# Weights as the stationary operand for the first modulation, and moving operands of high and low columns side by side

## The reference

```python
silu_c = jax.nn.silu(c)[:, None, :]
silu_cc = jax.nn.silu(c_ctx)
for i in range(DEPTH):                      # DEPTH = 4
    sh_a, sc_a, g_a, sh_m, sc_m, g_m = jnp.split(silu_c @ mod_w[i] + mod_b[i], 6, axis=-1)
    h_lat = modulate(x_lat, norm_mix_g[i], sh_a, sc_a)
    ...                                     # the same for the context with silu_cc
    y_lat = fourier_mixer | diff_attention_mixer | mla_mixer
    x_lat = x_lat + g_a * y_lat
    x_lat = x_lat + g_m * sq_relu_mlp(modulate(x_lat, norm_mlp_g[i], sh_m, sc_m), mlp_w1[i], mlp_w2[i])
```

## Time and profile before

| what | value |
|---|---|
| median of three runs | 2016.28 us (2011.03 to 2016.95) |
| the profiled execution's own time | 2013.53 us |
| its span, first to last instruction | 2011.8 us |
| mean granted clock of TensorE | 0.984 |
| PE, DVE, ACT busy | 1921.9, 1531.0, 1018.4 us |
| bytes moved, mean rate | 346.67 MB, 172 GB/s |

### The profile page before, as it was taken

The page is one execution under the profiler, slowest core; times in us unless marked ns, Lnnn a source line. Parts: engine busy times, 40 slices in busy tenths (PEclk is TensorE's granted clock), DMA queues, the critical chain, the costliest instruction groups (busy, mean ns, idle before and its releaser), DMA issues.

```text
span 2011.8 us, 31051 instructions
## 1 busy us (share of the span) xinstructions
PE 1921.9 (96%) x11602; PEld 1684.5 (84%) x11602; DVE 1531.0 (76%) x2619; ACT 1018.4 (51%) x1721; POOL 22.5 (1%) x40
## 2 busy tenths in 40 slices
PE   6889999999999999999999777999999999999998
PEld 4687888889787888888888667999999999997886
DVE  3689888887667758777777588788887667876796
ACT  5353323245666656232333577655555546655685
POOL 0200000000000000000000100000000000000000
PEclk9999999999999999999999899999999999999999
DMA  7936455541211234557675220677645555426795
GB/s 291 321 119 232 165 209 188 188 168 48 84 64 63 67 112 139 169 186 244 236 244 158 58 73 27 227 268 261 207 135 189 168 169 168 134 67 236 260 354 195
DMA packets 265319, 346.67 MB, mean 172 GB/s; under 512 B 24167, under 2 KB 234962, under 8 KB 263778
## 3 DMA queue, kind: packets, MB, share of 16 engines
q1 hardware_dynamic: 265186, 344.90, 51.2%
HBM read 343.81 MB, written 1.06 MB: 171 GB/s over the span
## 4 chain that ended last, share of the span: by engine, by line
PE 75%; DVE 10%; ACT 6%; issue 5%; SPq 1%; DMA 1%; DVEq 0%; ACTq 0%
PE bank L1847 23%; PE bank L1848 23%; PE bank L1849 23%; PE bank L2663 2%; DVE w_lo L2818 2%; PE bank L2653 1%; ACT p_raw L1401 1%; ACT p_raw L1389 1%; DVE p_all L3297 1%; ACT norm L1157 1%; ACT w_hi L1064 1%; ACT mp_raw L1569 1%; DVE x L2886 1%; DVE neg_max L3306 1%; DVE norm L2844 1%
## 5 line engine op out<-in xcount | busy, mean ns | idle before, releaser
L2818 DVE TENSOR_TENSOR w_lo<-w_raw,w_hi 128x1024 fp32r<-128x1024 f32 x449 | 545.6, 1221 | 51.6 <-ACT w_hi L1064 24.9
L1064 ACT ACTIVATE w_hi<-w_raw 128x1024 fp32r<-128x1024 f32 x350 | 368.0, 1053 | 381.7 <-PE bank L1849 371.2
L1847 PE MATMUL bank<-h_hi,w_hi 128*128 128x512 f32 (+3 forms) x1360 | 466.9, 343 | 14.7 <-DVE w_lo L2818 8.6
L1848 PE MATMUL bank<-h_lo,w_hi 128*128 128x512 f32 (+3 forms) x1360 | 460.3, 338 | 0.0
L1849 PE MATMUL bank<-h_hi,w_lo 128*128 128x512 f32 (+3 forms) x1360 | 459.9, 338 | 0.0
L1847 PE MATMUL bank<-g_hi,w_hi 128*128 128x256 f32 (+1 forms) x1216 | 401.6, 330 | 7.2 <-DVE g_lo L3351 3.6
L1848 PE MATMUL bank<-g_lo,w_hi 128*128 128x256 f32 (+1 forms) x1216 | 399.6, 329 | 0.0
L1849 PE MATMUL bank<-g_hi,w_lo 128*128 128x256 f32 (+1 forms) x1216 | 399.5, 329 | 0.0
L1847 PEld LDWEIGHTS bank<-h_hi,w_hi 128*128 128x128 f32 x1360 | 257.9, 190 | 50.5 <-DVE w_lo L2818 10.8
L1849 PEld LDWEIGHTS bank<-h_hi,w_lo 128*128 128x128 f32 x1360 | 258.1, 190 | 27.7
L1848 PEld LDWEIGHTS bank<-h_lo,w_hi 128*128 128x128 f32 x1360 | 258.2, 190 | 26.4 <-issue 0.3
(11 more groups left out here) (535 smaller groups left out, 2832.0 us busy)
## 6 DMA issues: line engine op xcount, KB each, us to landing
w_raw<-in_mlp_w SPq DMA_DIRECT2D x128, 1024.0 KB, 5.4
mod_raw<-in_mod_t SPq DMA_DIRECT2D x80, 1024.0 KB, 7.3
w_raw<-in_w_expert_gate SPq DMA_DIRECT2D x34, 512.0 KB, 4.7
w_raw<-in_w_expert_up SPq DMA_DIRECT2D x34, 512.0 KB, 5.8
w_raw<-in_w_expert_down SPq DMA_DIRECT2D x17, 1024.0 KB, 5.7
first_raw<-in_mod_w SPq DMA_DIRECT2D x16, 1024.0 KB, 5.9
w_raw<-in_diff_w_qkv SPq DMA_DIRECT2D x12, 1024.0 KB, 5.2
w_raw<-in_fourier_w SPq DMA_DIRECT2D x8, 1024.0 KB, 7.9
```

Of the source, the lines that this page charges most:

```text
L1064: act.activation(split_panel(W_hi[n % RING], n), raw_panel(n), ACT.Copy).then_inc(s("w_hi"), 1)
L1847: pe.matmul(dst, w_hi, r_hi, start=start, stop=False)
L1848: pe.matmul(dst, w_hi, r_lo, start=False, stop=False)
L2818: dve.tensor_tensor(split_panel(W_lo[n % RING], n), raw_panel(n), split_panel(W_hi[n % RING], n).bitcast(F32), ALU.subtract).then_inc(s("p ...
```

## The change

It has two parts, and a third that follows from them.

1. First layer's modulation. 40 instead of 32 tiles are made on PE, now with the weights stationary (128x128, f32) and the two columns of `silu_c` moving, straight into the layout that DVE needs. There are three groups: tiles 0 to 15, 16 to 23 and 24 to 39. A load is 1 MB as before: 8 of the first group, 4 of the second (two k each), 8 of the third. `mod_unit` and `turn_first` go, as does ACT's copy; `first_unit` runs after every second step of `first_fourier` and twice behind each of the first four `fourier_w` panels. Only tiles 40 to 47 of layer 0 are still folded.
2. Latent-only products. `H_hi` and `H_lo`, and `G_hi` and `G_lo`, become halves of one tensor. `wide_product` sends high and low columns as one moving operand of 512 into the two halves of a bank, and the weight's low part times the high columns into the first half. `add_gated` then adds both halves to `X`, one after the other. It is used in `mlao`, `four3` and the second halves of `mlp2` and `mlp3`.
3. The folds are spread anew: none in the first stage, 112 in `mlp0`, 112 in `mlp1`, none in `mlp2`, and the loads with them.

```diff
-FIRST_GROUPS = 2
-FIRST_TILES = MOD_TILES // 3
+FIRST_GROUPS = [(0, 2 * KT, 1), (2 * KT, KT, 2), (3 * KT, 2 * KT, 1)]
+FIRST_LOADS = [(g, range(k, k + n)) for g, (_, _, n) in enumerate(FIRST_GROUPS) for k in range(0, KT, n)]
+FIRST_AT = [sum(of < g for of, _ in FIRST_LOADS) for g in range(4)]
...
-    tiles = [(0, t) for part in ("shift_m", "gate_m") for t in range(LATER_FIRST[part], LATER_FIRST[part] + KT)]
+    tiles = [(0, t) for t in range(5 * KT, MOD_TILES)]
...
-    take("first", [(0, 4)])
-    take("four0", enumerate([2, 2, 2, 2, 1, 1, 1, 1]))
...
-    for b, counts in enumerate(([0, 0, 1, 1, 1, 1, 2, 2] + some, 2 * some, 2 * some, some + [2, 1, 2, 1, 2])):
+    for b, counts in enumerate(([0, 1] + [2] * 14, [2, 2, 1, 2, 2, 1] + [2] * 10, [2, 2, 1, 2, 2, 1] + [2] * 10,
+                                [2, 2, 1, 2, 2, 1] + [2] * 6 + [1])):
         take(("mlp", 1, b), enumerate(counts))
-    for b in range(BLOCKS - 1):
-        take(("mlp", 2, b), enumerate([0] * KT + [1] * KT))
...
+        H_both = sb("h_hi", [P, 2, KT, TOK], F32R)
+        G_both = sb("g_hi", [P, 2, KT, TOK], F32R)
+        H_hi, H_lo, G_hi, G_lo = [v[:, i, :, :] for v in (H_both, G_both) for i in range(2)]
...
                 if layer == 0:
-                    block(0, "w0 w1 w2 m1 w3 m1 w4 w5 m1 w6 m1 w7 m1")
+                    block(0, "w0 w1 w2 m3 w3 w4 w5 w6 m1 w7 m1")
...
-                    block(0, "m3 w4 w5 w6 w7")
-                    block(1, "w0 m1 w1 m1 w2 m1 w3 m1 w4 w5 m1 w6 m1 w7 m1")
-                    block(2, "w0 w1 m2 w2 m1 w3 m2 w4 m1 w5 m2 w6 m1 w7 m2")
-                    block(3, "w0 m1 w1 m2 w2 m1 w3 m2 w4 m1 w5 m2 w6 m1 w7 m5")
+                    block(0, "m3 w4 w5 w6 w7 m1")
+                    block(1, "w0 m1 w1 m1 w2 m1 w3 m1 w4 m1 w5 m1 w6 m2 w7 m2")
+                    block(2, "w0 m1 w1 m2 w2 m2 w3 m2 w4 m2 w5 m2 w6 m2 w7 m2")
+                    block(3, "w0 m1 w1 m2 w2 m2 w3 m2 w4 m2 w5 m2 w6 m2 w7 m6")
...
-            load_first(range(KT, FIRST_UNITS))
+            load_first(range(FIRST_AT[1], FIRST_AT[2]))
             for u in range(2):
                 load_unit(PLAN.at["four0"]["unit"] + u, [(whole, four_w[u])])
             sp.wait_ge(s("u_lo"), 4 + GROUPS)
             for u in range(2, 4):
                 load_unit(PLAN.at["four0"]["unit"] + u, [(whole, four_w[u])])
+            load_first(range(FIRST_AT[2], FIRST_AT[3]))
             sp.wait_ge(s("c_all"), 16)
             spread_c()
-            for n in range(len(LATER_FIRST) * KT // MOD_PAIR // 2):
-                load_mod(next(mod_units))
             load_mlp(0)
...
+            def wide_product(dst, w_hi, w_lo, both, k, start, stop):
+                pe.matmul(dst[:, :].rearrange("p (h c) -> p h c", h=2), w_hi, both[:, :, k, 0:LAT], start=start, stop=False)
+                return pe.matmul(dst[:, 0:LAT], w_lo, both[:, 0, k, 0:LAT], start=False, stop=stop)
...
-            def mod_unit(u, g):
-                for j in range(4):
-                    ins = pe.matmul(mod_ps[32 * j:32 * (j + 1), 0:FIRST_PART], silu_c[:, u, :],
-                                    first_raw[n % FIRST_RING][:, j * FIRST_PART:(j + 1) * FIRST_PART],
-                                    start=(u == 0), stop=(u == KT - 1))
+            def first_unit(n):
+                g, ks = FIRST_LOADS[n]
+                tiles = FIRST_GROUPS[g][1]
                 pe.wait_ge(s(f"first_in{n % FIRST_RING}"), 16 * (n // FIRST_RING + 1))
+                for i, k in enumerate(ks):
+                    for t in range(tiles):
+                        w = slice((i * tiles + t) * P, (i * tiles + t + 1) * P)
+                        ins = pe.matmul(first_ps[g][:, 2 * t:2 * t + 2], first_raw[n % FIRST_RING][:, w], silu_c[:, k, :],
+                                        start=(k == 0 and t == 0), stop=(k == KT - 1 and t == tiles - 1))
                 ins.then_inc(s("first_used"), 1)
...
-                    mod_unit(n, 1)
+                    if n % 2:
+                        first_unit(FIRST_AT[1] + n // 2)
                 t = t0 + 4 * KT + 2
                 for m in range(4):
                     panel_product(n0 + m, t + m, H_hi, H_lo, slice(0, TOK), ready=lambda k: pe.wait_ge(s("four_lo"), k + 1))
-                    if m == 0:
-                        turn_first(1)
+                    for u in (2 * m, 2 * m + 1):
+                        first_unit(FIRST_AT[2] + u)
...
+                            if late:
+                                wide_panel(p0 + j, t0 + j, G_both, b, made)
+                            else:
+                                panel_product(p0 + j, t0 + j, G_hi, G_lo, slice(0, n_cols), b, made)
...
+                    if streams == 1:
+                        dve.scalar_tensor_tensor(X[:, m, c], bank[t % BANKS][:, LAT:TOK], gate, X[:, m, c],
+                                                 ALU.mult, ALU.add).then_inc(s("x_low"), 1)
+                        dve.wait_ge(s("x_low"), later(at + 1 - X_AT["mlao"], i, step))
+                    ins = dve.scalar_tensor_tensor(X[:, m, c], bank[t % BANKS][:, c], gate, X[:, m, c], ALU.mult, ALU.add)
                 ins.then_inc(s("x_done"), 1)
```

More of the change, by code:

```diff
@@ L491, in build_program @@
         subln = sb("subln", [P, 1])
-        silu_c = sb("silu_c", [P, KT, 32])
+        silu_c = sb("silu_c", [P, KT, 2])
         silu_t = sb("silu_t", [P, 2, KT])
@@ L508, in build_program @@
         mod_prod = sb("mod_prod", [P, D])
-        c_rows = sb("c_rows", [2 * KT, P], over=at["mod_prod"] + 4 * FIRST_PART)
+        c_rows = sb("c_rows", [2 * KT, P], over=at["mod_prod"])
         mod_end = base
@@ L1174, in boundary @@
                 root(name, LAT, 0)
-                if name == "mlp0":
-                    act.wait_ge(s("mod_folded"), folds_through(0, 4 * KT - 1))
                 act.wait_ge(s("scales_mix" if name.startswith("mix") else "scales_mlp"), layer + 1)
@@ L1849, in split_product, with wide_panel @@
                 return pe.matmul(dst, w_lo, r_hi, start=False, stop=stop)
+            def wide_product(dst, w_hi, w_lo, both, k, start, stop):
+                pe.matmul(dst[:, :].rearrange("p (h c) -> p h c", h=2), w_hi, both[:, :, k, 0:LAT], start=start, stop=False)
+                return pe.matmul(dst[:, 0:LAT], w_lo, both[:, 0, k, 0:LAT], start=False, stop=stop)
+            def wide_panel(n, t, both, i=None, ready=None):
+                if isinstance(i, int):
+                    n, t, i = n + i * MLP_TILES, t + i * MLP_TILES, None
+                pe.wait_ge(s("panel_ready"), later(n + 1, i, MLP_TILES))
+                wait_bank(t, i)
+                for k in range(KT):
+                    if ready:
+                        ready(k)
+                    w = slice(k * P, (k + 1) * P)
+                    ins = wide_product(bank[t % BANKS], W_hi[n % RING][:, w], W_lo[n % RING][:, w], both, k, k == 0, k == KT - 1)
+                ins.then_inc(s("tile_done"), 1)
             def wait_bank(t, i=None, step=KT):
@@ L2155, in _ @@
             for u in range(KT):
-                mod_unit(u, 0)
+                first_unit(u)
                 if u == KT - 1:
@@ L2872, in boundary @@
                 lat, con = slice(0, LAT), slice(LAT, TOK)
-                def folds(m):
-                    return {"mlp0": ("four0", m), "mix1": (("mlp", 0, BLOCKS - 1), KT + m)}.get(name, (None, m))
                 def gated(m, streams):
@@ L2895, in boundary @@
                         add_square(name, TOK, m - 1)
-                    mod_folds(*folds(m))
+                    if name == "mix1":
+                        mod_folds(("mlp", 0, BLOCKS - 1), KT + m)
                 split_lo_at(n0 + 4 + AHEAD)
@@ L2899, in boundary @@
                 add_square(name, TOK, 3)
-                mod_folds(*folds(4))
                 for m in range(5, KT):
@@ L2903, in boundary @@
                     add_square(name, LAT, m - 1, 0)
-                    mod_folds(*folds(m))
                 add_square(name, LAT, KT - 1, 0)
+                if name == "mlp0":
+                    first_read(2)
                 if name == "mix1":
@@ L3006, in mod_finish, with add_gated @@
                                          ALU.mult).then_inc(s(("scales_mix", "scales_mlp")[half]), 1)
-            def add_gated(m, t, xn, layer, gate_at, streams, i=None, step=0):
+            def add_gated(m, t, xn, layer, gate_at, streams, i=None, step=0, at=None):
+                at = xn if at is None else at
                 dve.wait_ge(s("tile_done"), later(t + 1, i, MLP_TILES))
@@ L3079, in first_fourier @@
                 add_bias(0, 2)
-                mod_folds("first", 0)
                 boundary(p0, t + 4 * KT + 2, X_AT["four0"], "mlp0", 0, (0, 2 * KT))
@@ L3116, in fourier @@
                     split_lo_at(p0 + m + AHEAD)
-                    add_gated(m, t + m, 0, layer, 2 * KT, streams)
+                    add_gated(m, t + m, 0, layer, 2 * KT, streams, at=X_AT[name] + m)
                     if m:
@@ L3401, in output_added @@
```

(2 more changed lines are left out.)

105 lines of the change are left out of this document (35 added, 70 removed).

## The result

The changed kernel takes 2107.42 us in the median (2104.74 to 2111.02, four runs) against 2015.65 for the kernel before beside it. The ratio is 1.0462, with a 95% interval from 1.0446 to 1.0478: slower by 91.8 us. The prediction said 81 us slower (2095 us), with a range from 2036 to 2125. The profiled execution took 2106.70 us, with a span of 2105.0.

A forecast was written before the change was run, and what follows sets the result against it. PE was taken to bound the kernel, busy 96% of 2011.8 us. First stage and norm plus 87 us, wide operands minus 6, gave plus 81: 2013.5 + 81 = 2095 us, range 2036 to 2125.

The forecast's parts named there:

- a clock that changes inside the stage: First stage: PE's clock is partly full, partly half; 2095 us, own range 2070 to 2112, chance 0.52.
- Full clock: First rival, first stage: dense products between the narrow units keep the clock at 1.00; 2038 us, chance 0.18.
- half throughout: Rival, first stage: half clock throughout the narrow stretches; plus 112 us, 2121 us, chance 0.2.
- a cheap matmul: Rival, first modulation: weight load hidden or short, only the two columns count, 0.055 us a record; 2002 us, chance 0.03.
- a bound `mlp1`: Rival, `mlp1`: folds or loads bind it, at worst 31 us, likelier 10 to 15; 2110 us, chance 0.06.
- The price of a record: First modulation: 640 narrow records at 0.112 us, 71.7 us where 19 were; 0.205 us each at half clock.
- The sum, by time: First stage added up stretch by stretch: group 0, transform, panels, half outputs; 86 us later there, 87 with the norm.
- The wait of 4.20 us: PE's wait for `four_w` in the first stage: goes, because its first load is issued after 9 units, not 13.
- Part 2: Folds moved out of the first stage and from `mlp2` to `mlp1`, plus 31 us of DVE in `mlp1`: cost nothing.
- Part 1: Wide operands in layers 2 and 3: 640 steps save 8.8 us, borders cost 3; minus 6, between minus 8.8 and 0.
- I charge 3 us for the four borders: Last blocks of `mlp2` and `mlp3`, `mlao`, `four3`: second add delays the next norm's last columns; 3 us, between 0 and 8.
- The length of DVE's round: Last block of `mlp3`: DVE's round grows from 2.61 to 3.1 us against a panel of 2.77; 8 panels slip by 2.6 us.

The follow-up runs named there:

- the run in the old form: Changed kernel with `silu_c` stationary in four strips and weights moving, three 256-column products per wide one, first two `fourier_w` loads early: 2007.66 us, ratio 0.9969.
- the run with 128: Changed kernel with 128 moving columns (zero-padded `silu_c`) instead of 2 in groups 0 and 1, group 2 keeping 2: 2072.31 us, ratio 1.0289.
- the run with the later folds as before: The run in the old form, with 88 folds in `mlp1` and 24 in `mlp2` instead of 112 and none: 2005.95 us, ratio 0.9963.
- Part 1 alone: Kernel before with only the wide operands and the split `add_gated`; first modulation and folds as before: 2017.8 us, ratio 1.0016.
- the run of Parts 2 and 3 alone: Changed kernel with three products of 256 columns for each wide one and without the second add: 2104.52 us, ratio 1.0443.

## Why the prediction was right, and where its sizes were off

**The direction and the cause** were right. Of its cases the likeliest came true, a clock that changes inside the stage. That the form of the matmul makes the loss is shown by the run in the old form, and that the few moving columns keep the clock low by the run with 128. Full clock (2038), half throughout (2121), a cheap matmul (2002) and a bound `mlp1` (2110) did not.

**The price of a record**, 0.112 us, is right: 0.109 at full clock in the run with 128 columns. At the low clock 0.195 to 0.209 were measured (0.205 taken). That 2, 32 and 128 columns do not differ refutes the case in which only the moving columns count. It doesn't by itself tell a load from a fixed cost of each record; the row with one stationary column, 0.06, speaks for the load, and no run tests it. The prediction named the Trainium skill (TensorE: Matmul & The Clock Gate, "Back-to-back issue gap") for an estimate of 0.025 us; the trace has four times that. The same section says that its table is for a single matmul without a budget for the weight load and counts too little at few columns, which the prediction left out.

**The clock.** The windows after show 0.59 to 0.69 with PE busy throughout. The rule of the Trainium skill (TensorE: Matmul & The Clock Gate, "Why this matters for your kernels"), that an engine kept busy without gaps holds the full clock, does not agree with this. By it the time would be that of the first rival, 2038. What the run with 128 columns adds is the cause. The loads, their number and their order are the same, and the three waits ahead of the stage nearly so (4.1, 3.6 and 1.8 us; 4.9, 3.2 and 1.5 in the changed kernel). More columns move and are written, and the clock is 1.00. Which of the two counts, moving or writing, can't be told apart here.

**The sum, by time.** Group 0 ended at 79.65 us (84.4 forecast), because two of its eight units ran mostly at full clock (3.8 and 4.1 us from start to start, the slow ones 6.7). The transform took 35.76 us (36.2 forecast, as the middle between 25.8 and 46.6, so the agreement is partly luck). Panels 0 to 3 with group 2 took 71.31 (67.9), since the clock was low for more of them. The wait for `h` behind them ended at 226.35 us, 85.2 us later than its twin at 141.19; the forecast was 87. Two slips in the rivals changed nothing: the full-clock case counts 28.3 us for a transform of 25.8, and the cheap case comes to 2001, not 2002. The wait of 4.20 us went, as forecast, and so did those for `w_lo` and the squares.

**Part 2** was charged nothing. In the trace after `mlp1` is 1.0 us longer; the run with the later folds as before differs by 1.7 us, inside what can be told.

**Part 1 is the step that failed in size**, the term "I charge 3 us for the four borders". The second add costs 10.0 us in the traces and 9.3 by the medians, not 3: 7.2 us of waits and some 1.7 of half clock behind one of them. The steps save about 6.5 us once the fall of the clock in the trace before is taken off (8.8 forecast). So the part costs about 3 us (3.7 by the medians alone, 1.8 and 2.2 between the marks of the two traces), where a gain of 6 was forecast. The length of DVE's round was forecast rightly (3.1 us; it is 3.05), and so was where it hurts. What was missed: the first border, out of `mlao`, where a round was thought to fit just barely, loses too. With Part 1 alone PE waits 2.18 us for `w_lo` there and 2.05 at the end of `mlp3`, since DVE splits the next weights only behind the late residuals. And a wait was priced by its length, without the clock behind it.

**Where the whole time went**, by marks in the two profiled executions (2011.8 and 2105.0 us, 93.2 apart): 85.2 us up to the wait for `h`; 1.1 more to the end of `mlp1` (its norm's sum starts at 1113.22 and 1199.49 us); 2.1 in the attention of `mla`; 2.2 in the stretch that Part 1 touches; 2.6 behind it, in the experts. In `mla` and the experts the code is not changed. No run explains these 4.7 us. One execution of each kernel is compared, and such pairs differ by some 3 us: the run of Parts 2 and 3 alone reaches the first mark at 1354.7 us and the changed kernel, with the same instructions up to there, at 1351.6.

## What to carry to other kernels

A record with a full 128x128 stationary operand took 0.11 us at full clock here, with 2 columns moving or 128, and an f32 matmul has two of them: 0.22 us. For a product with two columns let the two columns be the stationary operand and the weights move: 16 tiles over one k took 1.06 us in strips and 3.5 us the other way round, before any loss of clock. And where narrow matmuls can't be avoided, look at the granted clock behind them: 35 of the 92 us lost here came back when the first two groups ran almost wholly at 2.4 GHz (1.00 and 0.96), and to break the narrow work into small pieces among dense work made it worse.

Before an instruction is added on an engine that "has room", look at the stretches where its results are waited for one by one. The second add did no harm in mid-block, and at the 32 of 80 panels where each residual is waited for it took back all that the wide steps gave.

A wait can cost more than its length. Behind waits of 2.18 and 4.20 us the clock was at half for over 3 us, and moving two loads to take the wait of 4.20 away gave 6.3. When two traces are compared, look for such falls first: behind the wait for `meta_sq` the clock fell in one execution and not in another, and that alone was 1.7 us.

## What was not expected of the hardware

Zeros made it faster. Moving 128 columns, 126 of them padding, in place of 2 took 35 us off the kernel, and 32 took 10 off. The finer mixture of narrow and dense work held the clock at 0.50 for 95 us without a break (0.69 for the coarse one).

In Part 1 the 512-column matmul came every 0.227 us in some panels and every 0.234 in others (a panel of 2.77 or 2.83 us) at the same granted clock. What decides between the two is open.
